# First layer's modulation in pieces of 256 columns, first weights in pairs of depths

## Chip, core and metric

The kernel runs on one core of one Trainium2 chip. The metric is the device time of one execution in microseconds (us). The engines are TensorE (PE in the profile, its weight loads PEld), VectorE (DVE), ScalarE (ACT), GpSimd (POOL) and SyncE (SP, which issues transfers).

## What is computed

Two blocks run on one sequence of 512 tokens of width 1024 in float32: a block of two layers (a gated MLP mixer, then an attention with three branches, each followed by a feed-forward part) and a third layer with two more kinds of attention. Cut to what matters here:

```python
def modulate(h, shift, scale):
    return h * (1.0 + scale[:, None, :]) + shift[:, None, :]

def gmlp_mixer(h, w_in, ln_g, ln_b, w_s, b_s, w_out):
    z = jax.nn.gelu(h @ w_in)
    u, v = jnp.split(z, 2, axis=-1)
    v = layer_norm(v, ln_g, ln_b)
    ...
    mixed = jnp.einsum('gts,bcsgd->bctgd', w, v) + b_s.T[:, :, None]
    return (u * mixed.reshape(B, T, SGU_WIDTH)) @ w_out

    # first_block
    c_act = jax.nn.silu(c)
    for layer in range(DEPTH):
        mod = c_act @ ada_w[layer] + ada_b[layer]
        sh1, sc1, g1, sh2, sc2, g2 = jnp.split(mod, 6, axis=-1)
        h = modulate(rms_norm(x, norm_g[layer, 0]), sh1, sc1)
        y = gmlp_mixer(h, ...) if layer == 0 else nsa_mixer(h, ...)
        x = x + g1[:, None, :] * rms_norm(y, norm_g[layer, 1])
        h = modulate(rms_norm(x, norm_g[layer, 2]), sh2, sc2)
        y = jnp.square(jax.nn.relu(h @ ff_w_in[layer])) @ ff_w_out[layer]
        x = x + g2[:, None, :] * rms_norm(y, norm_g[layer, 3])
```

The change lies in the first layer, from the start to the product `h @ w_in`: `mod` is a vector times a matrix of 1024 x 6144 (`ada_w[0]`), of which the first product needs the 2048 columns of `sh1` and `sc1`. The mixer's weights `w_s` are needed too: transposed, and multiplied once with the layer norm's bias.

## The kernel before

Depths: the 1024 inputs of a product are 8 depths of 128 (k = 0 to 7). A chunk is 512 output columns of a weight matrix over all 8 depths; its two halves of 4 depths (1 MB each) are units, `RAW[:, u]`. A float32 product is made of three matmuls of a high part and a remainder: ACT copies a unit to `WH` (`hi`, L730), DVE subtracts to get `WL` (`lo`, L1250), and in the same way `HIDh` and `HIDl` are the parts of the activations (`split`, L1514 and L1517). `three` (L2085) issues the three matmuls of one depth and one bank of PSUM. In the stage at the start every bank takes 128 tokens by 512 columns.

Modulation: 512 columns of `ada_w` for all 8 depths are loaded (2 MB), DVE multiplies each depth with its column of `silu(c)` and adds up (`mod_acc`, L1270: one instruction of 480 ns, seven of 752 ns, each dependent on the one before). What is left is a sum over 128 partitions. At the start (chunks 2, 0, 3, 1 of the modulation) PE makes it with four matmuls against a column of ones (`column`, L2249), and DVE turns it into coefficients `AB` (`coefs`, L1329). Later chunks of the first layer (4 and 5, the gate) are summed by POOL (`mod` in `pool_program`, L488), after which DVE adds bias and gain (`mod_post`, L1290).

The order of every engine is written out by hand; nothing is scheduled. In `head` (ACT L769, DVE L1350, PE L2242 to L2336) the first four depths wait for the modulation chunks 2 and 0 and the last four for 3 and 1; PE takes depths 0 to 3 of the first chunk, with the transposes of x (L2265), of `w_s` (L2302) and the bias product (L2313) in between, then depths 0 to 3 of the second chunk, then depths 4 to 7 of both. ACT moves the bias product to `MIXC` (L797, `mix_e`) after the first of these.

POOL works through a fixed list. The lines on which the prediction rests:

```python
        pool.wait_ge(mix_e, 2)
        pool.wait_ge(bs_in, 16)
        flat = lambda v: v.rearrange("p g t -> p (g t)")
        pool.tensor_tensor(flat(MIXC[:]), flat(MIXC[:]), flat(BS[:]), ALU.add).then_inc(mix_cr, 1)
        for _ in range(2):
            mod()
```

So POOL's first sum, of chunk 4, stands behind the addition to `MIXC`. Behind `mod_post` of that chunk DVE has: `BN_STATS` of the first values (L1532), `mod_acc` of chunk 5, `lo` of a unit, `mod_post`, the statistics and the normalization of `V` (L1548), `mod_acc` of chunk 6, two `lo`. SP loads the second half of the mixer's third chunk (`weight`, L314) only behind the bias row `GB` of chunk 5, which waits for that `mod_post` (`mod`, L343). PE sums chunk 6 by `mod_column` (L2341, L2348) before the mixer's first product (`mix`, L2357).

## Time and profile before

| | us |
|---|---|
| median of 3 runs | 1553.31 (1553.22 to 1553.75) |
| span of the profiled execution, first to last instruction | 1551.4 |
| PE busy | 1507.1 (97%) |
| DVE busy | 1095.7 (71%) |
| ACT busy | 692.6 (45%) |
| POOL busy | 286.1 (18%) |
| DMA bytes | 203.35 MB, mean 131 GB/s |

The page gives no time for the profiled execution beside its span; the median of the runs is 1.9 us above it, and that much is taken to lie around the span. PE's share of busy time is an average over stages. Starts are counted from the span's start. A float32 matmul that is not split into parts is recorded as two matmuls: four matmuls of `column` are eight records.

### The profile page before, as it was taken

The page shows a single profiled execution, that of the slowest core. Times are in us where ns is not written, and L with a number is a line of the kernel's source. Part 1 is how long each engine was busy: PE and PEld are TensorE (multiplying, and loading weights), DVE is VectorE, ACT ScalarE, POOL GpSimd, SP SyncE. Part 2 cuts the span into 40 slices and gives each one's busy share as a digit, 9 for nine tenths or more (in the row PEclk, how much of TensorE's full clock was granted, in tenths as well). Part 3 has the DMA queues.
Part 4 walks back from the last instruction along what each step waited for, and adds up shares of the span by engine and source line. Part 5 has one row for each costly group of instructions (what it writes and reads, how often), then busy time and mean ns, then how long its engine had stood idle before and what let it go on. Part 6 is the DMA issues. An engine that isn't in the chain of part 4 may idle for free.

```text
span 1551.4 us, 20894 instructions
## 1 busy us (share of the span) xinstructions
PE 1507.1 (97%) x8187; PEld 1252.2 (81%) x8187; DVE 1095.7 (71%) x1607; ACT 692.6 (45%) x1177; POOL 286.1 (18%) x230
## 2 busy tenths in 40 slices
PE   4999999999999999989999999999999999999998
PEld 3888888888888897977788988888888988677677
DVE  6798688889989764269885785556634824799775
ACT  3433551322214544357774642313233525887651
POOL 0200013223232000058870020111100011010210
PEclk9999999999999999999999999999999999999999
DMA  9675257578584315230001164443332232211101
GB/s 332 243 265 181 82 204 246 189 248 293 184 294 161 107 34 174 77 108 2 2 2 56 56 225 160 159 144 115 132 109 83 84 109 66 92 61 55 55 1 55
DMA packets 108808, 203.35 MB, mean 131 GB/s; under 512 B 6041, under 2 KB 13478, under 8 KB 108710
## 3 DMA queue, kind: packets, MB, share of 16 engines
q1 hardware_dynamic: 108710, 202.01, 38.2%
q8 instruction: 65, 1.06, 0.3%
q14 instruction: 33, 0.27, 0.1%
HBM read 199.90 MB, written 2.10 MB: 130 GB/s over the span
## 4 chain that ended last, share of the span: by engine, by line
PE 81%; DVE 10%; issue 3%; DMA 2%; ACT 2%; POOL 1%; SPq 1%; DVEq 0%; POOLq 0%; ACTq 0%
PE PS L2142 47%; PE PS L2095 20%; DVE MACC L1287 3%; PE PS L2477 3%; PE PS L2504 2%; DVE WL L1253 2%; PE PS L2467 2%; PE PS L2654 1%; PE PS L2166 1%; DMA MRAW<-in_ada_w_dram 1%; POOL MROW L494 1%; DMA X<-in_x_dram 1%; PE PS L2676 1%; PE PS L2469 1%; DMA RAW<-in_ff_w_in_dram 1%
## 5 line engine op out<-in xcount | busy, mean ns | idle before, releaser
L733 ACT ACTIVATE WH<-RAW 128x2048 fp32r<-128x2048 f32 (+1 forms) x111 | 208.2, 1886 | 362.4 <-DMA RAW<-in_ff_w_in_dram 223.5
L1253 DVE TENSOR_TENSOR WL<-RAW,WH 128x2048 fp32r<-128x2048 f32 (+1 forms) x107 | 269.4, 2540 | 123.3 <-ACT WH L733 123.1
L494 POOL PARTITION_ALL_REDUCE MROW<-MACC x26 | 123.3, 4743 | 601.8 <-DVE MACC L1287 514.5
L2142 PE MATMUL PS<-WH,HIDh 128*128 128x512 f32 (+1 forms) x576 | 217.4, 377 | 0.0
L2142 PE MATMUL PS<-WH,HIDl 128*128 128x512 f32 (+1 forms) x576 | 217.3, 377 | 0.0
L2142 PE MATMUL PS<-WL,HIDh 128*128 128x512 f32 (+1 forms) x576 | 217.3, 377 | 0.0
L2142 PE MATMUL PS<-HTh,WH 128*128 128x512 f32 (+1 forms) x520 | 202.5, 389 | 0.6 <-DVE WL L1253 0.6
L2142 PE MATMUL PS<-HTl,WH 128*128 128x512 f32 (+1 forms) x520 | 202.4, 389 | 0.0
L2142 PE MATMUL PS<-HTh,WL 128*128 128x512 f32 (+1 forms) x520 | 202.3, 389 | 0.0
L1287 DVE SCALAR_TENSOR_TENSOR MACC<-MRAW,CS,MACC 128x512 f32<-128x512 f32 x168 | 126.3, 752 | 8.6 <-DMA MRAW<-in_ada_w_dram 1.1
L2095 PE MATMUL PS<-HTh,WH 128*128 128x256 f32 (+1 forms) x384 | 123.8, 322 | 4.8 <-DVE WL L1253 4.5
L2142 PEld LDWEIGHTS PS<-WH,HIDh 128*128 128x128 f32 x576 | 108.3, 188 | 20.5 <-issue 0.2
L2142 PEld LDWEIGHTS PS<-WH,HIDl 128*128 128x128 f32 x576 | 108.3, 188 | 20.1
L2142 PEld LDWEIGHTS PS<-WL,HIDh 128*128 128x128 f32 x576 | 108.3, 188 | 20.1
L2095 PE MATMUL PS<-HTh,WL 128*128 128x256 f32 (+1 forms) x384 | 122.3, 319 | 0.0
L2095 PE MATMUL PS<-HTl,WH 128*128 128x256 f32 (+1 forms) x384 | 122.2, 318 | 0.0
L2142 PEld LDWEIGHTS PS<-HTh,WH 128*128 128x128 f32 (+1 forms) x520 | 97.1, 187 | 21.7 <-issue 1.0
L2142 PEld LDWEIGHTS PS<-HTh,WL 128*128 128x128 f32 (+1 forms) x520 | 97.1, 187 | 21.0
L2142 PEld LDWEIGHTS PS<-HTl,WH 128*128 128x128 f32 (+1 forms) x520 | 97.1, 187 | 20.5
L558 POOL TENSOR_SCALAR PB<-PB,SM 128x128 f32<-128x128 f32 (+3 forms) x93 | 93.5, 1013 | 19.6 <-DVE SM L1797 15.1
L942 ACT ACTIVATE RB<-PS 128x512 f32<-128x512 f32 x64 | 38.2, 597 | 130.7 <-PE PS L2142 108.4
L1630 DVE SCALAR_TENSOR_TENSOR SQ<-RB 128x512 f32<-128x512 f32 x64 | 44.1, 689 | 58.6 <-ACT RB L942 58.5
(344 smaller groups left out, 2971.8 us busy)
## 6 DMA issues: line engine op xcount, KB each, us to landing
MRAW<-in_ada_w_dram SPq DMA_DIRECT2D x44, 1024.0 KB, 7.4
RAW<-in_ff_w_in_dram SPq DMA_DIRECT2D x32, 1024.0 KB, 5.4
RAW<-in_ff_w_out_dram SPq DMA_DIRECT2D x32, 1024.0 KB, 5.1
RAW<-in_w_in_dram SPq DMA_DIRECT2D x16, 1024.0 KB, 5.3
MRAW<-in_w_ada_dram SPq DMA_DIRECT2D x12, 1024.0 KB, 8.5
RAW<-in_a_w_in_dram SPq DMA_DIRECT2D x8, 1024.0 KB, 9.7
MRAW<-in_kv_ada_w_dram SPq DMA_DIRECT2D x8, 1024.0 KB, 6.2
RAW<-in_kv_w_dram SPq DMA_DIRECT2D x6, 1024.0 KB, 5.1
```

Source lines behind the costliest of these rows:

```text
L494: pool.partition_all_reduce(MROW[:], MACC[:], P, RADD).then_inc(m_red, 1)
L558: pool.tensor_scalar(w, w, SM[:, c_:c_ + 1], None, ALU.mult).then_inc(a_ps, 1)
L733: act.activation(WH[:, wslot(u), 0:width(u)], RAW[:, u % 4, 0:width(u)], ACT.Copy).then_inc(w_hi, 1)
L942: act.activation(RB[:, k % 2, :], ps, ACT.Relu).then_inc(relu_rdy, 1)
L1253: dve.tensor_tensor(WL[:, u % 4, 0:width(u)], RAW[:, u % 4, 0:width(u)], WH[:, wslot(u), 0:width(u)].bitcast(F32), ALU.subtract).then_inc( ...
L1287: dve.scalar_tensor_tensor(out=acc, in0=src, scalar=vec[:, k:k + 1], in1=acc, op0=ALU.mult, op1=ALU.add).then_inc(m_acc, 1)
L1630: dve.scalar_tensor_tensor(out=SQ[:, k % 2, :], in0=RB[:, k % 2, :], scalar=1.0, in1=RB[:, k % 2, :], op0=ALU.mult, op1=ALU.mult).then_inc ...
L2095: mm = pe.matmul(po, a, b_, start=(k == 0 and i == 0), stop=(k == KT - 1 and i == 2), skip_group_check=True)
L2142: mm = pe.matmul(po, a, b_, start=(k == 0 and i == 0), stop=(k == KT - 1 and i == len(ops) - 1), skip_group_check=len(ops) > 3)
L2467: pe.matmul(out_, queries(qts[blk], e), k[:, of, g, 0:L], start=(k is KDh), stop=False, skip_group_check=True)
L2477: mm = pe.transpose(PS[0:rows_, 3 + u % 3, P * i:P * i + P], weights_of(u)[:, step * i:step * i + step], IDENT[:])
L2504: mm = pe.matmul(head(blk, h), VT[:, br, kt, HD * g:HD * g + HD], turned_of(of[h])[:, c_:c_ + P], start=False, stop=(br == 1 and kt == qts ...
```

## The change

- The modulation of the first product is loaded in eight pieces of 256 columns (`PIECE`, 1 MB each in two transfers with rows of 1 KB instead of 2 KB), in the order scale, shift, scale, shift, ... A pair of pieces serves two depths. DVE sums a piece with eight instructions of 256 columns (`head_acc`) in two halves (even and odd depths), which PE's eight matmuls against ones add up (`head_columns`). There are four sets of coefficients (`head_coefs`) instead of two.
- The first two weight chunks are loaded, split and used in pairs of depths (`first_weight`, `first_hi`, `first_lo`, `depth`): PE takes depths 2p and 2p+1 of both chunks before it goes on to the next pair.
- ACT writes the high part of a turned depth straight from PSUM (`scaled`), where DVE's cast L1514 did it; DVE keeps the subtraction.
- The parameter rows for `C1` and part of `C02` are issued by ACT; those for the rest of `C02` by SP, behind all weights of this stage. ACT's table for the square root is loaded early by a one-element instruction.
- The transposes of `w_s` and the bias product now stand at the last pair, four at a time in one bank.

On DVE, in the middle of `head`: the names are the tiles, `MRAW` and `M3a` the loaded columns of 512. Before:

```order
L1284 TENSOR_SCALAR MACC<-MRAW,CS 128x512 [waits m_in0,m_red]
L1287 SCALAR_TENSOR_TENSOR MACC<-MRAW,CS,MACC 128x512 [waits m_acc] x3
L1287 SCALAR_TENSOR_TENSOR MACC<-MRAW,CS,MACC 128x512 [waits m_acc,m_in1]
L1287 SCALAR_TENSOR_TENSOR MACC<-MRAW,CS,MACC 128x512 [waits m_acc] x3
L1253 TENSOR_TENSOR WL<-RAW,WH 128x2048 [waits w_hi]
L1284 TENSOR_SCALAR MROW<-M3a,CS 128x512 [waits m3_in0,m_red]
L1287 SCALAR_TENSOR_TENSOR MROW<-M3a,CS,MROW 128x512 [waits m_acc] x3
L1361 COPY MCOL<-PS 128x4 [waits m_red]
L1287 SCALAR_TENSOR_TENSOR MROW<-M3b,CS,MROW 128x512 [waits m_acc,m3_in1,m_red]
L1287 SCALAR_TENSOR_TENSOR MROW<-M3b,CS,MROW 128x512 [waits m_acc] x3
```

Now, for one pair of depths (`PIECE_85` and `PIECE_86` are two pieces):

```order
L1277 TENSOR_TENSOR WL<-RAW,WH 128x1024 [waits w_first_pair_hi]
L1380 SCALAR_TENSOR_TENSOR MACC<-PIECE_85,CS,MACC 128x256 [waits head_acc,head_columns_in21]
L1380 SCALAR_TENSOR_TENSOR MACC<-PIECE_85,CS,MACC 128x256 [waits head_acc] x3
L1277 TENSOR_TENSOR WL<-RAW,WH 128x1024 [waits w_hi]
L1377 TENSOR_SCALAR MROW<-PIECE_86,CS 128x256 [waits m_red,head_columns_in30]
L1377 TENSOR_SCALAR MROW<-PIECE_86,CS 128x256
L1380 SCALAR_TENSOR_TENSOR MROW<-PIECE_86,CS,MROW 128x256 [waits head_acc] x2
L1380 SCALAR_TENSOR_TENSOR MROW<-PIECE_86,CS,MROW 128x256 [waits head_acc,head_columns_in31]
L1380 SCALAR_TENSOR_TENSOR MROW<-PIECE_86,CS,MROW 128x256 [waits head_acc] x3
L1387 COPY MCOL<-PS 128x2x2 [waits m_red]
L1342 TENSOR_TENSOR SCT<-MCOL,C_68 128x2 [waits m_post]
L1344 TENSOR_TENSOR AB<-MCOL,C_68 128x2
```

What was one dependent string of eight instructions of 512 columns is two strings of eight of 256 columns, one for scale and one for shift, with two splits of weights in them, and the coefficients follow at once.

On PE, where the sums of a later modulation chunk stand. Before, in depths 0 to 3 of the first chunk:

```order
L2095 MATMUL PS<-WL,HIDh 128x512
L2095 MATMUL PS<-WH,HIDl 128x512
L2302 MATMUL PS<-IDENT,WSR 128x128 [waits x_raw,pool_consts]
L2302 MATMUL PS<-IDENT,WSR 128x128 x7
L2254 MATMUL PS<-ONES,MACC 128x1 [waits m_acc,x_raw]
L2254 MATMUL PS<-ONES,MACC 128x1 x3
L2095 MATMUL PS<-WH,HIDh 128x512 [waits tile_rdy]
L2095 MATMUL PS<-WL,HIDh 128x512
L2095 MATMUL PS<-WH,HIDl 128x512
```

Now, from the end of the first pair to the start of the second:

```order
L2329 MATMUL PS<-WH,HIDh 128x512 x2
L2329 MATMUL PS<-WL,HIDh 128x512 x3
L2288 MATMUL PS<-ONES,MROW 128x1 [waits x_scaled,head_acc]
L2288 MATMUL PS<-ONES,MROW 128x1 x3
L2288 MATMUL PS<-ONES,MACC 128x1 x4
L2329 MATMUL PS<-WH,HIDl 128x512 x3
L2294 MATMUL PS<-IDENT,V 128x128 [waits m_post,x_scaled]
L2294 MATMUL PS<-IDENT,V 128x128 x3
L2329 MATMUL PS<-WH,HIDh 128x512 [waits tile_hi,w_lo]
L2329 MATMUL PS<-WH,HIDh 128x512 x3
L2294 MATMUL PS<-IDENT,V 128x128 [waits x_scaled]
L2294 MATMUL PS<-IDENT,V 128x128 x3
```

PE's sum now waits for `head_acc` with three matmuls of the pair behind it, and the next pair's first depth needs the transposes and ACT's `tile_hi` that come after it.

On ACT, around the copies to `WST` and `MIXC`. Before:

```order
L789 ACTIVATE XR<-PS 128x512 [waits full] x4
L792 ACTIVATE WST<-PS 128x512 [waits mix_turned]
L792 ACTIVATE WST<-PS 128x512
L733 ACTIVATE WH<-RAW 128x2048 [waits w_in1]
L797 ACTIVATE MIXC<-PS 128x512 [waits mix_bias]
L797 ACTIVATE MIXC<-PS 128x512
L766 ACTIVATE RB<-XR,AB 128x512 [waits tile_rdy,x_raw,first_coefs]
L766 ACTIVATE RB<-XR,AB 128x512 [waits tile_rdy] x3
L733 ACTIVATE WH<-RAW 128x2048 [waits w_in3,m_acc]
L733 ACTIVATE WH<-RAW 128x2048 [waits w_in0]
```

Now:

```order
L765 ACTIVATE HIDh<-PS,AB 128x512 [waits full,first_coefs]
L769 ACTIVATE RB<-PS,AB 128x512 [waits tile_rdy]
L765 ACTIVATE HIDh<-PS,AB 128x512 [waits full]
L769 ACTIVATE RB<-PS,AB 128x512 [waits tile_rdy]
L759 ACTIVATE WH<-RAW 128x1024 [waits w_in3]
L791 ACTIVATE WST<-PS 128x512 [waits mix_turned] x2
L795 ACTIVATE MIXC<-PS 128x512 [waits mix_bias] x2
L726 ACTIVATE WH<-RAW 128x2048 [waits w_in0]
L887 ACT_TABLE_LOAD
L887 ACTIVATE V<-PS 128x512 [waits full] x4
```

The copies to `MIXC` were ahead of the last four depths; now they are behind all eight, and the first `WH` of the next chunk is behind them. POOL's own order is unchanged.

The diff, cut to its core:

```diff
-    XR = at("XR", [P, 4, T], F32, o_y)
-    M3 = [at("M3a", [P, 4, 512], F32, o_w + 24576), at("M3b", [P, 4, 512], F32, o_y + 8192)]
+    PIECE = [at(f"PIECE{i}", [P, KT, 256], F32, (o_mraw, o_mraw + 8192, o_y, o_y + 8192)[i]) for i in range(4)]
...
+    HEAD_BANK = (0, 1) + (3,) * 6
...
+        def first_weight(c_, pair):
+
+            u = 2 * c_ + pair // 2
+            src = a_w_in[0].rearrange("(k p) n -> p k n", p=P)[:, bass.ds(2 * pair, 2), bass.ds(D + 512 * c_, 512)]
+            dst = RAW[:, u, 1024 * (pair % 2):1024 * (pair % 2) + 1024].rearrange("p (k n) -> p k n", k=2)
+            sp.dma_start(dst, src).then_inc((wp_in, w_in)[pair % 2][u], 16)
+
+        def head_columns(p):
+
+            src = cols_of(ada[0], D * (1 - p % 2) + 256 * (p // 2), 256)
+            if p >= 4:
+                sp.wait_ge(h_acc, 8 * (p - 3))
+            for h in range(2):
+                sp.dma_start(PIECE[p % 4][:, 4 * h:4 * h + 4, :], src[:, 4 * h:4 * h + 4, :]
+                             ).then_inc(h_in[p % 4][h], 16)
...
+        for p in range(2):
+            head_columns(p)
+        for tt in range(TT):
+            load_x(tt)
+        for pair in range(4):
+            if pair:
+                head_columns(2 * pair)
+                head_columns(2 * pair + 1)
+            first_weight(0, pair)
+            first_weight(1, pair)
...
+        def scaled(k):
+
+            src = PS[:, HEAD_BANK[k], :]
+            act.wait_ge(full, 4 + k + 1)
+            act.activation(HIDh[:, k, :], src, ACT.Identity, scale=AB[:, 0, k:k + 1], bias=AB[:, 1, k:k + 1]
+                           ).then_inc(tile_hi, 1)
             if k >= 2:
                 act.wait_ge(tile_rdy, k - 1)
-            act.activation(RB[:, k % 2, :], src, ACT.Identity, scale=AB[:, 0, k:k + 1],
-                           bias=AB[:, 1, k:k + 1]).then_inc(done, 1)
+            act.activation(RB[:, k % 2, :], src, ACT.Identity, scale=AB[:, 0, k:k + 1], bias=AB[:, 1, k:k + 1]
+                           ).then_inc(x_ev, 1)
...
+            first_hi(0, 0)
+            for pair in range(4):
+                act.wait_ge(coef0, pair + 1)
+                scaled(2 * pair)
+                scaled(2 * pair + 1)
+                first_hi(1, pair)
+                if pair < 3:
+                    first_hi(0, pair + 1)
...
-            act.wait_ge(mix_b, 1)
             for i in range(2):
-                act.activation(MIXC[:, 4 * i:4 * i + 4, :].rearrange("p g t -> p (g t)"), PS[:, 2 + i, :], ACT.Copy
+                act.wait_ge(mix_b, i + 1)
+                act.activation(MIXC[:, 4 * i:4 * i + 4, :].rearrange("p g t -> p (g t)"), PS[:, 3, :], ACT.Copy
                                ).then_inc(mix_e, 1)
...
+            def head_acc(p, part):
+
+                for k in part:
+                    acc = (MACC, MROW)[p % 2][:, 256 * (k % 2):256 * (k % 2) + 256]
+                    src = PIECE[p % 4][:, k, :]
+                    if k % 4 == 0:
+                        dve.wait_ge(h_in[p % 4][k // 4], 16 * (p // 4 + 1))
+                    if k == 0 and p >= 2:
+                        dve.wait_ge(m_red, p // 2)
+                    if k < 2:
+                        dve.tensor_scalar(acc, src, CS[:, k:k + 1], None, ALU.mult).then_inc(h_acc, 1)
+                    else:
+                        dve.wait_ge(h_acc, 8 * p + k - 1)
+                        dve.scalar_tensor_tensor(out=acc, in0=src, scalar=CS[:, k:k + 1], in1=acc,
+                                                 op0=ALU.mult, op1=ALU.add).then_inc(h_acc, 1)
...
+            def head_coefs(i):
+
+                dst = MCOL[:, 0:16].rearrange("p (a c) -> p a c", a=2)[:, :, 2 * i:2 * i + 2]
                 dve.wait_ge(m_red, i + 1)
-                dve.tensor_copy(MCOL[:, 4 * ch:4 * ch + 4], src).then_inc(m_post, 1)
+                dve.tensor_copy(dst, PS[:, 3, 0:4].rearrange("p (a c) -> p a c", a=2)).then_inc(m_post, 1)
                 dve.sem_inc(m_c, 1)
                 n.mod += 1
+                dve.wait_ge(m_post, i + 1)
+                coefs(0, AB, 8, 0, C_NG, slice(2 * i, 2 * i + 2)).then_inc(coef0, 1)
+
+            def remainder(k):
+
+                dve.wait_ge(x_ev, k + 1)
+                dve.tensor_tensor(HIDl[:, k, :], RB[:, k % 2, :], HIDh[:, k, :].bitcast(F32), ALU.subtract
+                                  ).then_inc(tile_rdy, 1)
...
+            for pair in range(4):
+                remainder(2 * pair)
+                if pair < 3:
+                    head_acc(2 * pair + 2, range(4))
+                remainder(2 * pair + 1)
+                first_lo(1, pair)
+                if pair < 3:
+                    head_acc(2 * pair + 2, range(4, KT))
+                    first_lo(0, pair + 1)
+                    head_acc(2 * pair + 3, range(KT))
+                    if pair == 2:
+                        dve.wait_ge(m_red, 4)
+                        dve.tensor_copy(C02[:, P:P + PAR2], PS[:, 3, P:P + PAR2]).then_inc(cols, 1)
+                    head_coefs(pair + 1)
...
+        def head_columns(i):
+
+            pe.wait_ge(h_acc, 16 * i + 16)
+            if i:
+                pe.wait_ge(x_ev, 2 * i)
+            if i == 3:
+                pe.wait_ge(par2_in, 16 * 8)
+                pe.transpose(PS[:, 3, P:P + PAR2], PR2[:], IDENT[0:PAR2, 0:PAR2])
+            for j in range(4):
+                acc = (MROW, MACC)[j // 2]
+                for e in range(2):
+                    o = 256 * e + P * (j % 2)
+                    mm = pe.matmul(PS[:, 3, j:j + 1], acc[:, o:o + P], ONES[:], start=(e == 0), stop=(e == 1),
+                                   skip_group_check=True)
...
+        for pair in range(4):
+            k = 2 * pair
+            if pair == 0:
+                depth(0, 0)
+            else:
+                depth(0, k, (lambda: turn_later(k + 1), None, None))
+            if pair < 3:
+                depth(0, k + 1)
+                depth(1, k)
+                depth(1, k + 1, (None, lambda: head_columns(pair + 1), lambda: turn_later(k + 2)))
+            else:
+                depth(0, k + 1, (None, lambda: weights_turned(0), None))
+                depth(1, k, (lambda: weights_turned(1), None, lambda: bias(0)))
+                depth(1, k + 1, (None, None, lambda: bias(1)))
+        pe.wait_ge(mix_e, 2)
+        for k in range(KT):
+            mm = three(bank(4, 3), k, slice(3 * P, 4 * P), "B", HIDh, HIDl, 2 + k // 4)
```

## Rows read from the trace of the kernel before

**Rows 1.** The page's first line.
```profile
span 1551.4 us, 20894 instructions
```

**Rows 2.** View by stretches: us, busy of each engine, granted clock, DMA share, GB/s.
```profile
18.00:20.00 2.00, 0.00 (x0) 0.00 (x0) 1.92 (x4) 0.53 (x1) 0.00 (x0) 1.00 1.03 412
616.00:618.00 2.00, 2.00 (x16) 1.91 (x15) 0.20 (x1) 0.79 (x1) 0.00 (x0) 1.00 1.06 378
```

**Rows 3.** Chain of waits, 31 to 130 us: start us, us, what.
```profile
31.25 7.56 PE PS L2095 x24
...
83.33 21.76 PE PS L2142 x96
105.09 0.79 PE PS L2341 x8
105.88 3.68 PE PS L2357 x32
109.56 20.64 PE PS L2142 x91
```

**Rows 4.** Timeline of DVE: start us, us, instruction [idle before <-releaser].
```profile
8.98 0.49 DVE L1284 TENSOR_SCALAR MACC<-MRAW,CS 128x512 f32<-128x512 f32 x1 [3.36 <-DMA MRAW<-in_ada_w_dram]
9.50 5.55 DVE L1287 SCALAR_TENSOR_TENSOR MACC<-MRAW,CS,MACC 128x512 f32<-128x512 f32 x7
...
24.89 0.16 DVE L1333 TENSOR_TENSOR SCT<-MCOL,C 128x4 f32<-128x4 f32 x1
24.97 0.16 DVE L1335 TENSOR_TENSOR AB<-MCOL,C 128x4 f32<-128x4 f32 x1
...
30.41 0.69 DVE L1517 TENSOR_TENSOR HIDl<-RB,HIDh 128x512 fp32r<-128x512 f32 x1
...
32.09 1.22 DVE L1260 TENSOR_TENSOR WL<-RAW,WH 128x1024 fp32r<-128x1024 f32 x1
...
86.00 2.94 DVE L1253 TENSOR_TENSOR WL<-RAW,WH 128x2048 fp32r<-128x2048 f32 x1 [1.55 <-ACT WH L733]
...
97.59 5.55 DVE L1287 SCALAR_TENSOR_TENSOR MACC<-MRAW,CS,MACC 128x512 f32<-128x512 f32 x7
...
107.46 0.16 DVE L1577 COPY MCOL<-PS 128x4 f32<-128x4 f32 x1
```

**Rows 5.** DVE groups by form: xcount | busy us, mean ns | idle.
```profile
L2002 DVE SCALAR_TENSOR_TENSOR DB<-DB,SM,DB 128x256 f32<-128x256 f32 x4 | 1.9, 485 | 0.1
```

**Rows 6.** Timeline of PE, columns as for DVE.
```profile
13.59 0.48 PE L2246 MATMUL PS<-IDENT,PR 128*128 128x128 f32 x1 [8.28 <-DMA PR<-in_subln_g_dram]
...
15.20 1.84 PE L2254 MATMUL PS<-ONES,MACC 128*128 128x1 f32 x8 [0.88 <-DVE MACC L1287]
...
38.65 1.91 PE L2265 MATMUL PS<-IDENT,V 128*128 128x128 f32 x16
...
44.03 0.95 PE L2254 MATMUL PS<-ONES,MACC 128*128 128x1 f32 x8
```

**Rows 7.** ACT groups by form, 0 to 66 us.
```profile
L766 ACT ACTIVATE RB<-PS,AB 128x512 f32<-128x512 f32 x4 | 3.0, 775 | 1.2 <-PE PS L2265 0.7 <-DVE HIDl L1517 0.5
...
L797 ACT ACTIVATE MIXC<-PS 128x512 f32<-128x512 f32 x2 | 1.1, 596 | 2.3 <-PE PS L2313 2.3
```

**Rows 8.** Timeline of POOL, columns as for DVE.
```profile
50.81 3.27 POOL L510 TENSOR_TENSOR MIXC<-MIXC,BS 128x1024 f32<-128x1024 f32 x1 [21.85 <-ACT MIXC L797]
69.47 5.17 POOL L494 PARTITION_ALL_REDUCE MROW<-MACC  x1 [15.39 <-DVE MACC L1287]
84.55 3.23 POOL L494 PARTITION_ALL_REDUCE MROW<-MACC  x1 [9.90 <-DVE MACC L1287]
```

**Rows 9.** Timeline of SP, transfers issued.
```profile
3.77 0.96 SPq L340 DMA_DIRECT2D MRAW<-in_ada_w_dram  x2
...
76.99 4.03 SPq L324 DMA_DIRECT2D RAW<-in_a_w_in_dram  x2
```

307 lines of the change are left out of this document (118 added, 189 removed).

## Prediction

> **What bounds the kernel now.** I read the chain of waits first. From the first matmul of the first product at 31.25 us on it lies on PE nearly without a break: the second mixer product begins at 83.33, a modulation column is summed on PE at 105.09, the first mix product follows at 105.88, the next chunk starts at 109.56 [rows 3]. So the span of 1551.4 us [rows 1] is 31.25 us of preparation and then PE's work, and what shifts PE at 109.56 shifts the end. I take it one to one: from there to the end the chain releases everything, transfers too, from PE. The sum is made against the profiled span; the median of the runs, 1553.3, lies 1.9 above it.
>
> The second view is DVE's timeline, because DVE is the engine that feeds PE in this stretch. Before the start it waits for the first columns until 8.98 and then needs 0.49 + 5.55 = 6.0 us for each 512 columns [rows 4]. Behind the stage it is barely ahead: its sum for the column at 105.09 starts at 97.59 and is done at 103.1, its copy at 107.46 is what the fourth of four mix products waits for, and that one would start at 105.88 + 3/4 x 3.68 = 108.6 [rows 3, 4]. The slack is 1.0 us.
>
> The third view is POOL's timeline: an addition to `MIXC` of 3.27 us at 50.81, idle, and from 69.47 to 74.64 the first sum over partitions, of modulation chunk 4 [rows 8]. With that sum a fixed string on DVE begins (gate, statistics, chunk 5, split, gate, statistics, normalization, chunk 6, two splits, copy). It ends at 107.62 [rows 4], 33.0 us after POOL's sum, with one quarter of 3.68 on PE behind it: PE's next chunk can't start before POOL's sum + 34.0 us.
>
> **Term 1, the start.** All of what is loaded shrinks to what two depths need. Columns were issued at 3.77 as 1 MB and used at 8.98 [rows 4, 9], 5.2 later; half the bytes at the about 0.39 MB/us of this stage (412 GB/s in 18 to 20) [rows 2] take 1.3 less, so issued at 0.8 they are there at 4.7. `CS` needs the parameter rows, now on ACT's queue: I take 6.5 for DVE's first sum (4.7 to 9.0; the upper end is the row of before).
>
> A piece is two products and six multiply-adds of 256 columns. 256 columns of the latter took 485 ns [rows 5]; the product took 0.49 for 512; half of it would be 0.25, and by the ratio of the multiply-adds (0.485 to 0.75) it is 0.32, so I take 0.34. In a string in which each depends on the last, spacing is the full duration plus 0.04 (5.55 / 7 = 0.79). Here each depends on the last but one, and two independent instructions of 0.16 us stand 0.08 apart [rows 4]. I take 0.08 off each: 2 x 0.26 + 6 x 0.41 = 3.0, with one tail 3.1; bounds 3.0 and 8 x 0.53 = 4.2. On this the Trainium skill has a rule that speaks against the change: VectorE: DVE Perf Modes, section "The DRAIN you can't avoid", says that after an instruction the pipeline is flushed before a held next one starts, semaphore or not. By that rule a piece is 3.6, and the eight pieces would cost 4 us more; the overlapping pair at 24.89 and 24.97 disagrees for small ones, and no row shows it for 256 columns.
>
> Piece 0 ends at 9.6. Then DVE waits for the rows of `C02`, issued by ACT only after `CS`: landing between 9 and 13 (the late rows of before had PE wait until 13.59 [rows 6]); I take 11.5. Piece 1 ends at 14.6. PE's column sum is now eight matmuls, 16 records, where eight took 1.84 at the slow pace [rows 6]: 3.7. Coefficients 0.7 (a copy and two of 0.16 with their waits), two normalizations of x at an estimated 0.95 (between 0.69 for 512 columns and 1.22 for 1024), one half-size split 1.2 [rows 4]: 22.1. Together: first matmul at 22 instead of 31.25 (20 to 25). The squares on ACT, one table load shorter, and the weights, half as large, lie beside this.
>
> **Term 2, the pairs.** The number of large matmuls is the same 192, at 21.76 / 96 = 0.227 [rows 3]. But after each pair there is a loop through all engines that nothing covers:
> - DVE: two pieces 6.2, two half-size splits of 1.22 less overlap 2.3, two remainders of 0.69 [rows 4] 1.3, small waits 0.5: 10.3.
> - PE: the sum, 16 records at twice 0.95 [rows 6] = 1.8.
> - PE: three matmuls left of the pair 0.7, four transposes 4 x 1.91 / 16 [rows 6] with their tail 0.6; DVE's coefficients lie beside it.
> - ACT: `HIDh` and `RB`, 0.775 each [rows 7] less overlap 1.4, and DVE's next remainder starts. With semaphores: 14.7 us.
>
> PE's work in a pair is 42 x 0.227 + 1.8 + 0.9 = 12.2. So PE pauses 2.5 us in each loop, about 1.7 ahead of the sum and 0.8 ahead of `HIDh`. The cast that DVE loses is already out of these sums. The first loop is 14.2, since at the start 24 matmuls took 7.56 instead of 5.4 [rows 3] and fill the pause. Pair 3 starts at 22 + 14.2 + 14.7 + 14.8 = 65.7.
>
> From there: 66 matmuls 15.0, transposes of x and `w_s` 1.3, bias product 1.8, and the wait for the last `MIXC` copy (0.6 [rows 7]) and its semaphores 0.8: 18.9. The stage ends at 84.6 against 83.33. Between first matmul and end it was 52.1 and becomes 62.6: the gain of 9.3 at the start is spent, and 1.3 more.
>
> Transfers don't bind by my sum: 3 MB a pair at 0.35 to 0.38 MB/us is 8 to 9 us, well under 14.7. Rows of 1 KB moved at 378 GB/s in 616 to 618 [rows 2]; bounds for a slower ACT queue beside SP's are inside Term 1.
>
> **Term 3, POOL.** `mix_e` moves from 50.8 to 24 matmuls, 5.5 us, before the end of the stage, 79.1. POOL then does its addition, 3.3, and only then the sum: 5.17 or 3.23 [rows 8]; DVE is mostly idle then, as at 84.55, so 4.2. POOL's sum ends at 86.6, 2.0 after the stage, where it ended 8.7 before it. By the string of 34.0 PE's chunk begins at 120.6 instead of 109.56. PE can't hide it: its own work from 83.33 to 109.56 is 26.2. What the trace should show are three pauses: for the split of the half chunk that SP issues behind `mod_post` (14.2 after POOL's sum: 74.64 to 88.94 [rows 4]), so at 100.8 where PE is ready at 95.5; for chunk 6's sum (28.4 after) about 3.5; and 1.0 for the copy.
>
> Sum: 1.3 + (36.0 - 26.2) = 11.1 us. 1553.3 + 11.1 = 1564.4.
>
> The rest costs nothing: ACT's copies, the moved `w_s` selection on POOL (idle until then), SP's late parameter rows (in by 45, used after 60), and the first `WH` behind the `MIXC` copies, ready with its split at about 83.5, just before it is used at 84.6; with 1 us less cover it costs that 1 us.
>
> **Rivals.**
> - A, PE is fed in the pairs: pieces at their lower bound and the loop covered. Then the stage takes 52.1 from 22 and ends at 74; for it speaks only that DVE's work alone, 10.3, is less than PE's 12.2; against it that the loop is a chain. POOL's string still gives 74 + 36.0 = 110, so 0.5 slower than now: 1553.8.
> - B, the clock. In each pause and the thin matmuls after it PE is little used. The rows at 15.20 and 44.03 show what the slow pace costs: eight records 1.84 instead of 0.95 [rows 6], and eight large matmuls about 1.6 to 2.1 more [rows 3]. If PE falls to it in all three loops, the sum costs 1.8 more on the chain and the rest about 0.7: 3 x 2.5 = 7.5, so 1572. The granted clock reads 1.00 in every stretch shown [rows 2], and no pause of 2 us inside dense work is followed by slow ones in these rows. The Trainium skill, TensorE: Matmul & The Clock Gate, "Part 1: The HAM clock gate", has idleness bring the engine to 1.2 GHz; by that rule B would come if these pauses count as idle.
> - C, faster: the 9.3 us at the start reach the end. This needs both a covered loop and POOL's string off the path, that is, mix copies early enough or slack in the string that I don't see (`MRAW`, `GB` and weights arriving earlier could take up to the 3 us that DVE waited around 84 to 86 out of it [rows 4], and shortened pieces a little). It decides from the point where the stage ends below 73. It would give 1553.3 - 9.3 = 1544, at partial success 1549.
> - D, loading in half-size transfers with short rows is slower than thought, below 250 GB/s: piece 3 comes after 28 and pairs stretch by 1 to 3 each: 1568.
>
> **Chances.** Forecast 0.66, A 0.08, B 0.12, C 0.06, D 0.08. Piece time is the main uncertainty: 0.5 more per piece costs 3.5 us, 1.5 us each way at the start. So 1557 to 1573, which leaves out A, C and the far ends. What this measurement can't tell from no change is 0.2%, 3.1 us. Faster by more: 0.06 (C); within: 0.08 (A); slower: 0.86.
>
> **What would show it.** Right: first large matmul near 22, starts of the pairs 14 to 15 apart, PE's sum waiting for DVE, POOL's `MIXC` addition near 79 with the sum directly behind it, three pauses of PE between 95 and 121. Wrong: loops near 12 (A), large matmuls spaced 0.43 after each pause (B), DVE waiting for a piece (D), POOL's sum before the end of the stage (C).

## The result and the profile after

The changed kernel takes 1583.9 us (median of 4 runs, 1582.4 to 1585.4) against 1553.4: the ratio is 1.0186, with an interval of 1.0170 to 1.0202. The profiled execution has a span of 1581.4 us, 30.0 more than before [rows 1]. The sign of the forecast is right, the size (1564.4, range 1557 to 1573) is not.

PE's timeline of the changed kernel, the rows where something begins (columns as in [rows 6]):

```profile
9.61 0.41 PE L2272 MATMUL PS<-IDENT,PR 108*128 108x108 f32 x1 [9.61 <-DMA PR<-in_cmp_b_dram]
16.36 0.45 PE L2274 MATMUL PS<-IDENT,PR 128*128 128x128 f32 x1 [6.35 <-DMA PR<-in_b_ada_dram]
20.42 1.84 PE L2288 MATMUL PS<-ONES,MROW 128*128 128x1 f32 x8 [3.61 <-DVE MROW L1380]
...
27.91 2.04 PE L2329 MATMUL PS<-WH,HIDh 128*128 128x512 f32 x4 [0.81 <-ACT HIDh L765]
...
42.82 2.05 PE L2329 MATMUL PS<-WH,HIDh 128*128 128x512 f32 x4 [1.02 <-ACT HIDh L765]
...
60.14 2.04 PE L2329 MATMUL PS<-WH,HIDh 128*128 128x512 f32 x4 [1.02 <-ACT HIDh L765]
...
76.81 2.05 PE L2329 MATMUL PS<-WH,HIDh 128*128 128x512 f32 x4 [1.02 <-ACT HIDh L765]
...
91.85 0.50 PE L2123 MATMUL PS<-WH,HIDh 128*128 128x512 f32 x1 [0.69 <-ACT MIXC L795]
...
117.63 0.79 PE L2170 MATMUL PS<-HIDh,WH 128*128 128x512 f32 x1 [9.16 <-DVE WL L1261]
...
131.91 1.02 PE L2386 MATMUL PS<-ONES,MACC 128*128 128x1 f32 x8 [1.73 <-DVE MACC L1296]
```

The first large matmul runs at 27.91 (31.25 before). The pairs begin at 27.91, 42.82, 60.14 and 76.81, so the loops are 14.9, 17.3 and 16.7 us long. At 91.85 the last 24 matmuls of the stage begin, and it ends at 97.43, where it ended at 83.33 [rows 3].

PE at the turn from the first pair to the second (view by stretches: us, busy, granted clock, DMA share, GB/s):

```profile
40.00:42.00 2.00, 1.80 (x12) 1.00 1.08 378
42.00:44.00 2.00, 1.18 (x3) 0.53 0.88 235
44.00:46.00 2.00, 2.00 (x9) 0.50 1.01 350
46.00:48.00 2.00, 2.00 (x6) 0.50 1.12 354
48.00:50.00 2.00, 2.00 (x8) 0.76 0.91 352
```

From 42 to about 49 the granted clock is 0.50, that is the level of 1.2 GHz; four large matmuls take 2.05 there and 1.07 at full clock. The same happens from 59 to 66 and from 76 to 80. PE's sums over the columns, at 38.71, 55.93 and 72.59, ran at full pace (eight records in 0.95 to 1.05): the clock fell behind them. The view doesn't show every slow stretch: from 28 to 32 it reads 1.00, and four large matmuls take 2.04 and 1.91 there, so the pace of the records is the surer sign.

POOL's timeline:

```profile
91.88 2.40 POOL L503 TENSOR_TENSOR MIXC<-MIXC,BS 128x1024 f32<-128x1024 f32 x1 [41.11 <-ACT MIXC L795]
100.03 3.25 POOL L487 PARTITION_ALL_REDUCE MROW<-MACC  x1 [5.75 <-issue]
```

The chain of waits there (start, us, what):

```profile
91.88 2.38 POOL MIXC L503
94.28 5.75 issue
...
137.45 2.77 PE PS L2170 x12
```

Between the end of the addition at 94.28 and the start of the sum at 100.03 lie 5.75 us in which POOL waits for nothing that the profile shows; the only record of POOL there is this one, the first of its line (from the view of POOL's sum by source line: count, ns, first and last start):

```profile
L487 POOLq MODIFY_POOL_CONFIG  x4: 4/5/11, 94.2 to 844.9; - x4
```

The same view of the kernel before:

```profile
L494 POOLq MODIFY_POOL_CONFIG  x4: 4/6/13, 54.0 to 818.2; - x4
```

There the record stands at 54.0, right behind the addition too, and the sum at 69.47 waited for DVE anyway [rows 8]. PE's next chunk starts at 137.45 instead of 109.56. From there to the end it takes 1443.9 us, before 1441.8. The profile shows two short falls of the clock there that the kernel before does not have:

```profile
1408.00:1428.00 20.00, 17.77 (x79) 0.91 0.31 106
...
1488.00:1508.00 20.00, 16.17 (x77) 0.91 0.19 70
```

All ratios here are made of executions in the chip's fast state; left out as slow are one of 5366 us of the kernel without the addition and one of 2169 us of the kernel before beside it.

### The profile page after: what moved, and what is told of

Its sections match the earlier page's. It is cut to its first block, busy times and chain, and to the rows that moved or that the text cites. A ratio compares the mean times of both kernels' runs of the same rounds, so it can differ in the third digit from the quotient of the medians.

```text
span 1581.4 us, 21026 instructions
## 1 busy us (share of the span) xinstructions
PE 1523.1 (96%) x8219; PEld 1263.1 (80%) x8219; DVE 1096.2 (69%) x1641; ACT 695.5 (44%) x1185; POOL 283.5 (18%) x230
## 4 chain that ended last, share of the span: by engine, by line
PE 86%; DVE 5%; issue 4%; ACT 2%; DMA 1%; SPq 0%; POOL 0%; DVEq 0%; POOLq 0%; ACTq 0%
PE PS L2170 54%; PE PS L2123 17%; PE PS L2522 3%; PE PS L2549 2%; PE PS L2512 2%; PE PS L2699 1%; PE PS L2452 1%; PE PS L2194 1%; DVE WL L1261 1%; PE PS L2721 1%; PE PS L2514 1%; DMA BS<-in_a_b_s_dram 1%; PE PS L2613 0%; PE PS L2598 0%; DMA RAW<-in_a_w_in_dram 0%
## 5 line engine op out<-in xcount | busy, mean ns | idle before, releaser
L726 ACT ACTIVATE WH<-RAW 128x2048 fp32r<-128x2048 f32 (+1 forms) x108 | 202.4, 1885 | 361.7 <-DMA RAW<-in_ff_w_in_dram 221.0
L1261 DVE TENSOR_TENSOR WL<-RAW,WH 128x2048 fp32r<-128x2048 f32 (+1 forms) x104 | 263.0, 2552 | 126.3 <-ACT WH L726 126.2
L1296 DVE SCALAR_TENSOR_TENSOR MACC<-MRAW,CS,MACC 128x512 f32<-128x512 f32 x154 | 115.8, 752 | 7.6 <-DVE MACC L1296 0.5
L2170 PEld LDWEIGHTS PS<-HTh,WH 128*128 128x128 f32 (+1 forms) x520 | 97.1, 187 | 20.6
L551 POOL TENSOR_SCALAR PB<-PB,SM 128x128 f32<-128x128 f32 (+3 forms) x93 | 93.6, 1014 | 19.5 <-DVE SM L1825 15.1
```

Of the source, the lines that this page charges most:

```text
L551: pool.tensor_scalar(w, w, SM[:, c_:c_ + 1], None, ALU.mult).then_inc(a_ps, 1)
L726: act.activation(WH[:, wslot(u), 0:width(u)], RAW[:, u % 4, 0:width(u)], ACT.Copy).then_inc(w_hi, 1)
L1261: dve.tensor_tensor(WL[:, u % 4, 0:width(u)], RAW[:, u % 4, 0:width(u)], WH[:, wslot(u), 0:width(u)].bitcast(F32), ALU.subtract).then_inc( ...
L1296: dve.scalar_tensor_tensor(out=acc, in0=src, scalar=vec[:, k:k + 1], in1=acc, op0=ALU.mult, op1=ALU.add).then_inc(m_acc, 1)
L2170: mm = pe.matmul(po, a, b_, start=(k == 0 and i == 0), stop=(k == KT - 1 and i == len(ops) - 1), skip_group_check=len(ops) > 3)
```

## Experiments

All were compared with the kernel before on the same chip. There its own runs scattered more than in the first comparison (1552 to 1561 us, medians 1553.6 to 1556.4), so the small ratios have wide intervals, and I read the mechanisms off the profiles: first large matmul, end of the stage, start of PE's next chunk.

The next chunk is read from the chain of waits.

| kernel | ratio (95%) | first large matmul | next chunk |
|---|---|---|---|
| before | 1 | 31.25 | 109.56 |
| changed, again | 1.0198 (1.0174 to 1.0221) | 27.93 | 138.95 |
| sums first | 1.0178 (1.0152 to 1.0204) | 27.35 | 135.19 |
| C02 later | 1.0163 (1.0130 to 1.0196) | 24.73 | 138.20 |
| filled pause | 1.0176 (1.0151 to 1.0201) | 27.71 | 136.32 |
| pieces ahead | 1.0187 (1.0160 to 1.0214) | 27.77 | 143.22 |
| rows first | 1.0172 (1.0148 to 1.0197) | 23.44 | 132.03 |
| covered | 1.0148 (1.0124 to 1.0171) | 28.32 | 128.26 |
| no addition | 1.0143 (1.0119 to 1.0167) | 28.53 | 134.65 |
| all | 1.0062 (1.0040 to 1.0083) | 23.19 | 118.56 |
| combined | 1.0021 (1.0008 to 1.0034) | 22.55 | 113.81 |
| addition in a wait | 1.0010 (0.9999 to 1.0022) | 23.18 | 110.75 |
| interleaved | 1.0037 (1.0023 to 1.0050) | 23.77 | 116.44 |
| before, late addition | 1.0038 (1.0023 to 1.0052) | 30.97 | 116.99 |
| before, 3.5 later | 1.0029 (1.0018 to 1.0041) | 34.73 | 113.88 |
| before, 8 later | 1.0055 (1.0040 to 1.0071) | 39.20 | 118.26 |

**The changed kernel again.**

> The changed kernel once more, beside the other three of this group, so that they are compared on one chip. Expected: about 30 us above the kernel before on the same chip (ratio 1.0186), first large matmul at 27.9, pairs at 42.8, 60.1 and 76.8, POOL's first sum 5.7 behind the end of its addition.

As expected in the ratio, the start and the gap on POOL (5.57). Its pairs began at 27.93, 43.82, 60.53 and 78.12, so single loops differ by 1 us between executions. PE's timeline of it, at the second pair and at the sum behind it:

```profile
43.82 1.16 PE L2329 MATMUL PS<-WH,HIDh 128*128 128x512 f32 x4 [1.02 <-ACT HIDh L765]
...
55.62 1.05 PE L2288 MATMUL PS<-ONES,MROW 128*128 128x1 f32 x8 [2.23 <-DVE MROW L1380]
```

Behind the same pause of 1.02 the clock did not fall here. PE then waited 2.23 us for DVE's sum instead of 0.67, and this loop still took 16.7. Its profile had no fall of the clock behind 160 us, and took 1441.9 from PE's next chunk to the end.

### POOL's change of configuration

**Before, with a late addition.**

```diff
+        pool.wait_ge(m_acc, 8 * 5)
         pool.wait_ge(mix_e, 2)
```

> The kernel before, with one wait more: POOL's addition to MIXC waits for DVE's MACC of chunk 4 (about 69.3), so that it stands directly ahead of the first sum, as it does in the changed kernel. Theory of the configuration: addition 3.3 (2.4 to 3.3), 5.7 us with MODIFY_POOL_CONFIG, sum 3.2 to 5.2, which then ends at 80.7 to 83.5 instead of 74.64. The string behind it ends 6 to 9 later, less 1.0 of slack: 1558.4 to 1561.3. Rival: the 5.75 us in the changed kernel were a wait of another kind (for a transfer of that moment), then only the addition comes on top: the sum ends at 78 and the time is 1555.7.

POOL's timeline of it:

```profile
69.44 4.37 POOL L511 TENSOR_TENSOR MIXC<-MIXC,BS 128x1024 f32<-128x1024 f32 x1 [40.75 <-DVE MACC L1288]
79.57 3.25 POOL L494 PARTITION_ALL_REDUCE MROW<-MACC  x1 [5.76 <-issue]
```

The same 5.76 us now stand in the kernel before, behind the same addition, and the sum ends at 82.82 instead of 74.64. The time rises by 0.23 to 0.52% (3.6 to 8.1 us), between the medians by 6.8. The mechanism is shown: a sum over partitions behind an ordinary POOL instruction costs 5.7 us of its own, which the kernel before hid in a wait. PE's next chunk came 7.4 us later, for the change of kind and the addition together.

**The sums first.**

```diff
+        for _ in range(2):
+            mod()
         pool.wait_ge(mix_e, 2)
         pool.wait_ge(bs_in, 16)
         pool.tensor_tensor(flat(MIXC[:]), flat(MIXC[:]), flat(BS[:]), ALU.add).then_inc(mix_cr, 1)
-        for _ in range(2):
-            mod()
```

> The changed kernel, with POOL's two sums over partitions (chunks 4 and 5) ahead of its addition to MIXC. Theory: POOL's string decides, and of it the part that stands behind the addition: 2.4 us of addition and 5.75 us between its end at 94.28 and the sum's start at 100.03, in which MODIFY_POOL_CONFIG is the only record. With the sums first, the configuration is changed while POOL waits, the first sum starts when DVE's MACC is done (89.4) and ends at 92.7 to 94.6 instead of 103.3. With the 34.2 us that lie between it and PE's next chunk that chunk starts at 127 to 129 instead of 137.5: about 9 to 10.5 us less, 1573 to 1575. Rival: the transfers set that string (DVE waited for columns of MRAW until 133.6), and then PE's next chunk stays near 133 to 137: 1579 to 1584.

POOL's timeline of it:

```profile
89.72 3.25 POOL L487 PARTITION_ALL_REDUCE MROW<-MACC  x1 [38.68 <-DVE MACC L1296]
...
118.85 2.44 POOL L505 TENSOR_TENSOR MIXC<-MIXC,BS 128x1024 f32<-128x1024 f32 x1 [8.71 <-issue]
```

DVE's, with the split ahead of the gate and the normalization:

```profile
94.83 2.29 DVE L1261 TENSOR_TENSOR WL<-RAW,WH 128x2048 fp32r<-128x2048 f32 x1 [5.26 <-ACT WH L726]
...
116.77 5.07 DVE L1576 TENSOR_SCALAR V<-V,SM,ST 128x1024 f32<-128x1024 f32 x4
```

POOL's sum was done at 92.97 as expected, but the next chunk came only 2.3 earlier. Three things took the place of the wait. DVE's split ahead of the gate waited until 94.83 for ACT's `WH`, which stands behind the `MIXC` copies (the prediction had this split ready just in time, at no cost). DVE's normalization took 5.07 instead of 2.98 while POOL's addition ran beside it. And PE ran its sum and the first mix products at the slow clock (7.2 us for 4.5). The change back to ordinary instructions also costs: the addition began 8.7 us after the second sum.

**No addition.** POOL's addition of b_s is left out, so the output lacks that term; ACT's high part of the next chunk goes ahead of the `MIXC` copies.

```diff
-        pool.tensor_tensor(flat(MIXC[:]), flat(MIXC[:]), flat(BS[:]), ALU.add).then_inc(mix_cr, 1)
...
+            hi(4)     # ACT
             for i in range(2):
                 act.wait_ge(mix_b, i + 1)
```

> The changed kernel without POOL's addition of b_s to MIXC (so the output lacks that term), and with ACT's high part of the next chunk ahead of the MIXC copies. With the sums only put first, PE's next chunk came 2.3 earlier, not 10: DVE waited until 94.8 for that high part, the late addition ran beside DVE's normalization (5.1 instead of 3.0) and the clock fell at the sum and the mix products. Theory: without all three the string has its 34 us again: first sum done at 92.7, next chunk of PE at 127 to 128.5 instead of 137.5, the time 8 to 10 below the changed kernel (1574 to 1576). Rival: the string has another bound (transfers of MRAW and RAW), and the chunk comes at 132 or later: 1579 or more.

The stage ended at 102.2 here (loops of 15.3, 19.8 and 18.0), 4.8 later than in the changed kernel, yet the next chunk came 2.8 earlier: 7.6 of the 8 to 10 are there, counted from the stage's end. POOL's sum ended at 99.47, and the string behind it took 35.2. So the absolute forecast missed, because the loops are not of fixed length; the string of 34 to 35 us held.

### The start

**C02 later.**

```diff
+            head_acc(1, range(KT))
             dve.wait_ge(full, 4)
             dve.tensor_copy(C02[:, 0:P], PS[:, 5, 0:P]).then_inc(ev_d, 1)
...
-            head_acc(1, range(KT))
```

> The changed kernel, with DVE's copy of C02 (which waits for the parameter rows that landed at about 16.3) behind the second piece instead of ahead of it. Theory: the start is late by that wait; DVE then does the piece from 13.6 to 16.6, the sum on PE starts at about 17.1 instead of 20.4, and the first large matmul at 24.5 instead of 27.9. If what follows is a loop of fixed length, the end comes 3.4 earlier too: about 1580.5. Rival: the transfers, which run at 350 to 400 GB/s without a pause until 34, are next: DVE waits for its pieces in the first loop, the first matmul is earlier but the second pair starts near 42 as now, and the time is 1583 to 1584.

The first large matmul came at 24.73, 3.2 earlier, but the second pair at 40.40, the third at 59.61 and the fourth at 76.72, where it was at 76.81: the loops gave it all back. DVE was not waiting for transfers, as the rival had it; its waits there are for `RB` (2.17) and for PE's sum (2.96). Between the ratios lie 3.6 us, but the intervals overlap, so the time says nothing.

**Rows first.**

```diff
+        first_rows(C_C, as_rows(c[0]))     # SP, seven transfers of C1, ahead of head_columns
...
-        rows(PR1, C_C, as_rows(c[0]), par1_in)     # ACT
...
+        rows(PR0, B_L[0], ...)     # ACT, C02's rows now ahead of CS
```

> The changed kernel, with the seven transfers of C1's parameter rows issued by SP ahead of the pieces, and the three of C02's by ACT at once instead of behind CS. Theory: the rows came late (9.6 and 16.3) because they ran beside the 1 MB pieces; alone they are there in about 2 us, as in the kernel before (PE idle until 5.3 there). CS at about 6, pieces from 8 and 11 on without a wait in between, first large matmul at 22.6 to 24 instead of 27.9, and the end 4 to 5 earlier. Rival: the start is then set by x and the first weights, which are issued 2 later (first matmul 26 or more), and the end moves by less than 2.

PE's timeline of it:

```profile
15.28 1.84 PE L2293 MATMUL PS<-ONES,MROW 128*128 128x1 f32 x8 [9.77 <-DVE MROW L1385]
...
23.44 2.05 PE L2334 MATMUL PS<-WH,HIDh 128*128 128x512 f32 x4 [0.81 <-ACT HIDh L777]
```

Shown: issued ahead of the pieces, the rows are early, and the first large matmul comes at 23.44, 4.5 earlier, inside my forecast for this run and near the 22 of the prediction. Beside the pieces of 1 MB they were there at 9.6 and 16.4. The pieces beside them made the difference, not the queue: here the rows of `C02` went on ACT's queue from 0.79, the pieces from 3.77, and the rows were used at 5.08; in the changed kernel the rows of `C1` went on the same queue from 0.79, the pieces from 0.80, and the rows were used at 9.61. Those of `C02` were issued there only at 10.37, behind `CS`. The next chunk came 6.9 earlier than in the repetition beside it: 4.5 are the start, 2.2 the loops.

### The pairs

**A filled pause.**

```diff
                 depth(1, k + 1, (None, lambda: head_columns(pair + 1), lambda: turn_later(k + 2)))
+                for j in range(4):
+                    pe.matmul(bank(4, j % 3), HIDh[:, k + 1, 0:P], WL[:, 2 + (k + 1) // 4, ...], start=False, ...)
```

> The changed kernel, with four more large matmuls (of the last depth again, into the same banks, so the sums are not the reference's) behind the transposes at the end of each of the first three pairs, where PE paused 1.02 us for ACT's HIDh. Theory of the clock: the pauses made the granted clock fall to 0.5 (42 to 49, 60 to 66, 76 to 80), in which some 12 large matmuls took 0.45 us each and not 0.23. Filled, the clock stays at 1.00, the second and third loop take about 14.7 instead of 17.3 and 16.7, the stage ends 4.5 to 6 us earlier, and so does all: 1578 to 1580. Rival: not the pause but the thin work around it (sum and transposes) lowers the clock, so the fall comes as before and the time stays 1583 to 1585; or DVE's chain sets the loops anyway, and PE only waits longer for its sum (3 us at 53 and 70): 1582 or more.

PE's timeline of it, second loop:

```profile
41.58 1.18 PE L2372 MATMUL PS<-WL,HIDh 128*128 128x512 f32 x4
42.84 1.16 PE L2329 MATMUL PS<-WH,HIDh 128*128 128x512 f32 x4
...
54.65 1.05 PE L2288 MATMUL PS<-ONES,MROW 128*128 128x1 f32 x8 [2.24 <-DVE MROW L1380]
```

The clock did stay at full speed at 42.84 (1.16 for four instead of 2.05). But now PE waited 2.24 us for DVE's sum at 54.65, and then the clock fell. The loops were 15.1, 18.0 and 16.2: no gain. So neither theory holds alone. The loop through DVE is as long as the slow PE was: whichever of them is faster waits for the other. Behind the wait of 2.24 the slow clock came back; behind the one of 1.42 ahead of the third loop's sum (72.67) it did not.

**Pieces ahead.**

```diff
-                remainder(2 * pair)
                 if pair < 3:
                     head_acc(2 * pair + 2, range(4))
+                remainder(2 * pair)
```

> The changed kernel, with DVE's first half of the next piece ahead of the first remainder of a pair (it waited 2.2 us there for RB), and nothing else. Theory of the chain: DVE's part of each loop is 1.5 shorter; where PE waited for the sum (0.7 to 2.2 in the second and third loop) that wait goes, 2 to 4 us in all. Theory of the clock alone: the falls at the start of the pairs stay, since PE's pause for HIDh stays, and the loops stay at 15 to 17: less than 1 us.

The ratio is that of the changed kernel: the clock theory's forecast held, the chain's did not. The profile is of one of its longer executions (its runs reach from 1580 to 1591), with loops of 15.2, 19.9 and 18.1 and the slow clock at each turn; PE still waited 2.09 for the sum in the second loop and paused 1.02 for `HIDh` in each. Moving DVE's work alone changes nothing while PE's sum and transposes stand where they are.

**Covered.**

```diff
-                depth(1, k + 1, (None, lambda: head_columns(pair + 1), lambda: turn_later(k + 2)))
+                depth(1, k + 1, (lambda: head_columns(pair + 1), lambda: turn_later(k + 2), None))
...
             for pair in range(4):
-                remainder(2 * pair)
+                first_lo(0, pair)
                 if pair < 3:
                     head_acc(2 * pair + 2, range(4))
-                remainder(2 * pair + 1)
-                first_lo(1, pair)
+                else:
+                    mod_part(range(2))     # chunk 4's sum, in three parts
+                remainder(2 * pair)
...
```

> The changed kernel, with another order in the pairs: DVE does the low part of the next weights and the first half of the next piece before the remainders, in the 2 us in which it waited for RB; PE makes the sum and the transposes one third of a depth earlier, so that large matmuls cover DVE's coefficients and ACT's HIDh; chunk 4's sum on DVE is cut in pieces and put in its waits of the last pair. Theory: the loop through DVE, PE and ACT made the pairs 14.9, 17.3 and 16.7 long, partly by pauses after which the granted clock fell to 0.5. Now DVE has 9.9 in a loop and the rest of the chain 2.6, PE 12.2: pairs of 12.5 to 13.2 each, no clock at 0.5, the stage ends 10 to 11 earlier, and so does the time: 9 to 11 us below the changed kernel. Rival: the transfers or POOL's string hold it: pairs of 12.5 but pauses of the same sum later, gain under 4.

PE's timeline of it:

```profile
28.32 2.04 PE L2352 MATMUL PS<-WH,HIDh 128*128 128x512 f32 x4 [0.81 <-ACT HIDh L765]
...
42.46 1.16 PE L2352 MATMUL PS<-WH,HIDh 128*128 128x512 f32 x4 [0.32 <-ACT HIDh L765]
...
55.75 1.16 PE L2352 MATMUL PS<-WH,HIDh 128*128 128x512 f32 x4 [0.32 <-ACT HIDh L765]
...
68.94 1.16 PE L2352 MATMUL PS<-WH,HIDh 128*128 128x512 f32 x4 [0.32 <-ACT HIDh L765]
```

Shown: pairs of 14.1, 13.3 and 13.2, pauses of 0.32 instead of 1.02, no slow clock at the three turns (only at the start, as before, by the pace of the records), the next chunk 10.7 earlier than in the repetition. What the order of the same instructions costs in these three loops is then 8 us against the first execution of the changed kernel (40.6 for 48.9) and 10 against the repetition (50.2). POOL's pause of 5.76 stayed, and PE waited 9.18 for it.

**All.** The edits of covered, rows first and C02 later, `hi(4)` ahead of the `MIXC` copies, and on POOL:

```diff
+        mod()
         pool.wait_ge(mix_e, 2)
...
-        for _ in range(2):
-            mod()
+        mod()
```

> All together: the rows first, C02's copy behind the second piece, the covered order of the pairs with chunk 4's sum spread over DVE's waits, POOL's addition between its two sums (so that its 5.7 us of configuration fall into the wait for chunk 5), and ACT's high part of the next chunk ahead of the MIXC copies. Theory: first large matmul at 23, pairs of 12.7, last pair at 61, end of the stage at 80 to 82 (83.3 in the kernel before), POOL's first sum at 70 and done at 73 to 75 (74.6 before), so PE's next chunk at 107 to 110 and the time within 3 us of the kernel before, on either side. Rival: of the 30 us some are in what none of these edits touches (slow clock later, transfers), then it stays over 1.005 of the kernel before.

POOL's timeline of it:

```profile
72.73 3.25 POOL L499 PARTITION_ALL_REDUCE MROW<-MACC  x1 [22.67 <-DVE MACC L1381]
82.58 2.40 POOL L516 TENSOR_TENSOR MIXC<-MIXC,BS 128x1024 f32<-128x1024 f32 x1 [6.60 <-issue]
92.06 4.10 POOL L499 PARTITION_ALL_REDUCE MROW<-MACC  x1 [7.08 <-issue]
```

The first sum ended at 75.98, but the addition between the sums cost a change of configuration both ways, 6.60 and 7.08 us, and held up the sum of chunk 5, for which DVE waited 3.14 us until 96.19. Before that DVE's split ahead of the first gate had waited until 76.05 for ACT's high part, so that the gate began at 78.26. From POOL's first sum to PE's next chunk it took 42.6 us instead of 34. The ratio of 1.0062 is the rival's (over 1.005), but not for its reasons: my place for the addition was wrong.

**Combined, and the addition in a wait.** Against the version before (all): no addition on POOL; PE's sum another third earlier; on DVE the low part of the next weights behind the second piece; w_s turned early in the last pair. In the first version DVE adds b_s as it takes `MIXC` out of PSUM, in the second in place behind `mod_acc` of chunk 5:

```diff
-                depth(1, k + 1, (lambda: head_columns(pair + 1), lambda: turn_later(k + 2), None))
+                depth(1, k, (None, None, lambda: head_columns(pair + 1)))
+                depth(1, k + 1, (lambda: turn_later(k + 2), None, None))
...
                 mod_acc(a_mods[i][0][0])
+                dve.tensor_tensor(flat(MIXC[:]), flat(MIXC[:]), flat(BS[:]), ALU.add).then_inc(mix_cr, 1)
             lo(4 + i)
```

> The rows first, the covered order in the pairs, with PE's sum one third of a depth earlier still and the low part of the next weights on DVE during that sum, PE's turning of w_s and the bias product early in the last pair, and no addition on POOL: DVE adds b_s as it takes MIXC out of PSUM, so POOL's sums follow each other with no change of configuration between. Theory: start 23.2, pairs 14.4, 12.2 and 12.2, last part 18.1 to 19: stage end 80 to 81 (83.3 in the kernel before), POOL's first sum done at 72 to 73, next chunk at 106.5 to 107.5, 2 to 3 us below the kernel before (ratio 0.998 to 0.9985). Rival: DVE with 10.8 us of work and the waits of the chain still makes pairs of 13.2: stage end 83 to 84, ratio 1.000 to 1.002. Third: slow clock later on, as in all kernels of this kind so far: 2 us more.

> As the combined version, but ACT again takes MIXC out of PSUM, and DVE adds b_s in place in the 1.6 us in which it waited for ACT's next high part (88.7 to 90.2), instead of before the first gate, where it held the gate from 75.2 (POOL's sum done) to 78.9. Theory: the gate starts at 75.2 to 75.5, the string of 34 us ends at 109.5, no pause ahead of PE's sum at 105 and so no slow clock there: next chunk at 109.3 to 110 instead of 113.6, ratio to the kernel before 0.999 to 1.001. Rival: the string is held elsewhere (ACT's high part of the next chunk later than 72), chunk at 112 or more, ratio 1.002 as in the combined version.

DVE's timeline of the first, the second addition and the gate:

```profile
76.09 0.69 DVE L1449 TENSOR_TENSOR MIXC<-PS,BS 128x512 f32<-128x512 f32 x1 [1.50 <-PE PS L2386]
...
78.89 0.69 DVE L1304 TENSOR_TENSOR GB<-GB,MROW 128x512 f32<-128x512 f32 x1
```

Of the second, the gate and the addition:

```profile
75.35 0.68 DVE L1308 TENSOR_TENSOR GB<-GB,MROW 128x512 f32<-128x512 f32 x1
...
85.40 1.22 DVE L1598 TENSOR_TENSOR MIXC<-MIXC,BS 128x1024 f32<-128x1024 f32 x1
```

In the first the gate waited for the second addition and the split behind it, from 75.21 to 78.89, and the next chunk came at 113.81. Its pairs took 14.1, 13.9 and 14.6 (14.4, 12.2 and 12.2 expected). In the second the gate began at 75.35 and the chunk came at 110.75. It has the early start (23.18), a stage that ends at 81.8, 1.5 before the old one, and a ratio of 1.0010 (0.9999 to 1.0022): no difference from the kernel before is shown. That is the best that I found on this change. No version beat the kernel before.

**Interleaved.** Against the version with the addition in a wait. `each` holds what follows each large matmul of the depth: two small ones or one transpose.

```diff
-                depth(1, k + 1, (lambda: turn_later(k + 2), None, None))
+                depth(1, k + 1, each=two + [None, turn_first] + [... turn_one(k + 2, tt) for tt in (1, 2, 3)] + [None])
```

> As the version with the addition in DVE's wait, with the eight small matmuls of PE's sum and the four transposes behind it set between large matmuls of the pair's last depth (two small ones, one large), so that PE has no stretch of 3 us with only small ones. In the combined version PE had no pause in the pairs at all, yet the granted clock fell at 48 and at 61. Theory: the small matmuls, during which PE does little, lower the clock. Spread out, it stays at 1.00 in the pairs, which are then 12.3 to 12.8 each after the first, stage end 81 to 82, next chunk at 107 to 108, ratio 0.998. Rival: the falls come from elsewhere and stay: stage end 83 to 84, ratio about 1.000.

In the combined version the view shows no pause of PE over 0.2 us in the pairs, and yet (stretches as above):

```profile
46.00:48.00 2.00, 2.00 (x16) 0.94 1.13 350
48.00:50.00 2.00, 2.00 (x6) 0.50 1.03 394
50.00:52.00 2.00, 2.00 (x9) 0.71 1.04 387
```

So a fall came without a pause that the view shows, behind PE's sum (16 small records from 44.84). The next version has the same order of instructions up to there; its clock fell once, at 47, and not at 61: a fall there is likely, not certain. That the small matmuls cause it is not shown: in the kernel before, 16 and again 16 small records in a row (38.65, 43.16) were followed by no fall. Interleaved, the clock held through the first two turns of pairs and fell in the third, but the transposes came later, PE paused 0.79, 0.79 and 0.76 for `HIDh`, and the pairs took 15.7, 13.6 and 15.4. It lost 0.27% against the version without, so it does not settle what keeps the clock up at no cost.

### The stretch that the change does not touch

**Before, later by six and by fourteen clears.**

```diff
+        for i in range(6):     # or 14
+            if i:
+                pool.wait_ge(late, i)
+            pool.memset(UT[:, 0, :], 0.0).then_inc(late, 1)
...
+        sp.wait_ge(late, 6)
         rows(PR1, C_C, as_rows(c[0]))
```

> The kernel before, with SP's first transfer held back by six clears of a buffer on POOL, one after the other (about 3.5 us); nothing else is moved. If a shift goes to the end one to one, the first large matmul and the end move by the same 3.5. Theory of the late clock: from PE's next chunk to the end the kernel before takes 1441.8, most of the others 1444 to 1446, with one to four short falls of the granted clock at 680 to 1500 where the kernel before has none; whether they come hangs on when the same pauses of PE come, not on the change. Then here too the end moves by 1 to 4 more than the start, with such falls in the records. Rival: they come from the change's own work; then the stretch from PE's next chunk to the end stays 1441.8 here.

> The same with fourteen clears (about 8 us). Theory of the late clock: start 8 later, end 8 to 12 later, and the falls at other places or in another number than with six. Rival: end 8 later within 0.5.

The first, by stretches, where before has 1.00 in all four:

```profile
680.00:700.00 20.00, 17.16 (x114) 0.91 0.00 1
1360.00:1380.00 20.00, 17.78 (x83) 0.91 0.24 88
1400.00:1420.00 20.00, 17.77 (x82) 0.91 0.14 52
1460.00:1480.00 20.00, 17.03 (x79) 0.91 0.31 107
```

The first large matmul moved by 3.5 and 8.0, PE's next chunk by 4.3 and 8.7: the 24 matmuls of the start took 8.39 and 8.34 us instead of 7.56, because the slow pace lasted longer into them. In the profiled execution of the first, the rest took 1448.8 instead of 1441.8, with four falls, 7.0 us or 1.75 each. That of the second had one fall and 0.7 us. So falls of this size come without any work of the change.

That a delay causes them is not shown. The medians rose by 4.3 and 8.7 us (1560.26 and 1564.61 against 1555.93), with intervals of 2.8 to 6.4 and 6.2 to 11.0. That is just what the next chunk had moved, so on average the shift went to the end one to one. And the kernel before, with nothing moved, took 1552.3 to 1559.6 on this chip, at mean granted clocks of 1.000 to 0.995: the falls come and go from one execution to the next. The profile of the kernel before that all is compared with is one that had none up to its last 20 us; the 2.1 us that the changed kernel lost late, and its repetition did not (1441.9), are of this kind.

## Why the prediction was wrong, step by step

The 18.7 us between the profiled run (1583.1; the median is 0.8 above it) and 1564.4 are made of these terms, up to rounding:

| step | predicted | measured | off by |
|---|---|---|---|
| Term 1, first large matmul | 22 | 27.91 | +5.9 |
| Term 2, from there to the end of the stage | 62.6 | 69.5 | +6.9 |
| Term 3, stage end to the end of POOL's sum | 2.0 | 5.85 | +3.9 |
| the string to PE's next chunk | 34.0 | 34.2 | +0.2 |
| from there to the end, one to one | 0 | 2.1 | +2.1 |
| what lies around the span | 1.9 | 1.7 | -0.2 |

Term 3 put POOL's change from the addition to the sum at nothing, without a reason, and it took 5.75 us. Terms 1 and 2 had the right path and were too small by 5.9 and 6.9 us.

- **Term 1** failed at its input, the parameter rows: I let `CS` be ready for a first sum at 6.5 and `C02` at 11.5, with the row of before as the upper bound. On ACT's queue, beside 1 MB pieces, they were there at 9.6 and 16.4, outside that bound. The upper bound came from a kernel in which the rows went first. The piece was right: 10.60 to 13.59, 3.0 us. The column sum was right too (3.5 at the slow pace, 3.7 predicted). By the flush that the Trainium skill, VectorE: DVE Perf Modes, section "The DRAIN you can't avoid", gives for a held next instruction, the piece would have been 3.6; the same section lets one that is not held start earlier. The trace shows the second case for two interleaved strings: 3.0, as the overlap read off the small instructions had it.
- **Term 2** has the right chain, but its DVE term and its clock were mis-sized. The loops came to 14.9, 17.3 and 16.7 for 14.2, 14.7 and 14.8, and the last part to 20.6 for 18.9. From DVE's first remainder to the end of its last piece the second loop took 12.5 for the 10.3 of the prediction. DVE's and POOL's timelines there:

```profile
47.24 0.69 DVE L1396 TENSOR_TENSOR HIDl<-RB,HIDh 128x512 fp32r<-128x512 f32 x1 [1.85 <-ACT RB L769]
...
49.33 2.51 DVE L1380 SCALAR_TENSOR_TENSOR MACC<-PIECE,CS,MACC 128x256 f32<-128x256 f32 x4
...
49.63 1.14 POOL L497 TENSOR_SCALAR_AFFINE_SELECT WSR<-WSR 128x1024 f32<-128x1024 f32 x1 [47.81 <-DMA WSR<-in_a_w_s_dram]
```

1.85 is a wait for the second `RB` of the pair, which hangs on a transpose behind four large matmuls at the slow clock; at full clock, in the repetition, that wait was 0.54. Another 0.84 is one multiply-add that took 1.32 instead of 0.48 beside POOL's selection on w_s (four took 1.67 elsewhere), which the prediction had called free; the kernel before paid it at its start (a split of 2.12 instead of 1.22 at 27.92).

Rival B, which I gave 0.12, came true on top of the forecast by its sign, the clock at the turn of all three pairs, but not by its price: it put 1.8 of 2.5 us per loop on PE's sum, and in this execution the sums ran at full pace (1.8, as in the forecast); the slow clock hit the first matmuls of each pair, and through them the second `RB`. Where PE waited about 2 us for the sum, as in the run with the pieces ahead (2.09), the sum itself came slow (1.73 for eight records) and the loop took 19.9. I had judged B by rows of dense work, in which no stretch holds 16 small records, a pause and four transposes in a row. The Trainium skill, TensorE: Matmul & The Clock Gate, "Part 1: The HAM clock gate", has idleness bring the clock down; here it fell behind pauses of 1.02 us, held behind the same pause in the repetition, and fell in the combined version with no pause in the view, so these traces don't settle what makes it fall. The filled pause shows that the clock alone is not the cause of the long loops either; the covered order shows that the order is.
- **Term 3** put the addition and the sum one behind the other without what lies between. The addition was 2.4 for 3.3 and the sum 3.25 for 4.2, 1.9 better, and the 5.75 us of changed configuration were missing. The price could be read before: the Trainium skill, GPSIMD Engine Reference, section 2.1 "Instruction dispatch", gives a load of about 6 us for the first call of a freshly loaded kernel, measured from the `MODIFY_POOL_CONFIG`, with no instruction to be seen. The trace agrees in size (5.75, 5.76), and shows that it is paid again at a later change of kind. The row of that record at 54.0, right behind the addition, was in the trace of before.
- **The string** was right to 0.2 us, and PE made the three pauses forecast for it: 9.16 for 5.3 (the 3.9 by which POOL's sum was later), 1.73 for 3.5 (behind the first pause PE ran at the slow clock from 117.6 to 120.4 by the pace of the records, which took part of it), and 0.57 for 1.0.
- **"One to one to the end"** held for the medians of the two delayed versions (4.3 and 8.7). In single profiled executions falls of the clock added 0 to 7 us.
- **D** did not happen: the profile shows no wait of DVE for a piece in the pairs. **C** was not reached: even with every repair the stage ends 1.5 earlier, and the time is the same.

## What to carry to other kernels

A step that is moved on an engine whose instructions come in two kinds needs the price of the change between them, and one must look whether that price is now hidden in a wait. Splitting a stage into smaller rounds puts a full turn through all engines behind each; before it is worth it, the order inside the round must leave PE large matmuls to do during the turn. A rival that only adds to the forecast (here the clock) is not an alternative to it, and can come on top. Its price times its chance belongs into the sum; that would have been only 0.9 us here (0.12 of 7.5), so what failed was the chance, taken from rows that did not look like the new stage. And small transfers that something waits for go ahead of the large ones; here it was the order of issue that counted, not the queue.

## What the hardware showed that I had not expected

- POOL's change between ordinary instructions and the sum over partitions costs 5.6 to 5.8 us ahead of the sum behind an addition, 7.1 in one case, and 6.6 to 8.7 on the way back. Its record stands at the end of the instruction before (54.0 and 94.2), also where POOL then waits for data, and the sum of the kernel before started at 69.47 with no delay of its own, so a wait can hide it.
- DVE's normalization of 128x1024 in place took 5.07 for four instead of 2.98 beside POOL's addition. The Trainium skill, SBUF — State Buffer, section "SBUF: two separate sides", has the two engines share one pair of ports, which one holds at a time; the 2.1 us lost beside an addition of 2.4 agree with that, as do the 0.84 us lost beside the selection on w_s.
- The granted clock fell twice in the combined version (0.50 from about 48 to 51 and from 61 to 65) while the view shows PE busy all the time. Falls of 1 to 2 us each come far behind the change, in the delayed kernel before too; a difference of a few us between two single profiles can be these alone.
